# Three of eight sample-attention chains moved into the last prompt-attention phase, their loads reordered, and the later tokens' outputs computed first

## What is computed

```python
h = rmsnorm(x, pre_w)
q_sb, k_sb, v_sb, g_sb, q_dl, k_dl, v_dl, g_dl = in_projection(h, w_in)   # 1024 -> 4096
# stick-breaking: a = exp(log_sigmoid(z) + sum over later keys of log_sigmoid(-z))
o_sb = stick_breaking(q_sb, k_all, v_all, q_pos, sb_b)
# dilated: three windows with ALiBi, joined by their denominators
o_dl = combine_by_denominator(outs, lses)
y = concat(headnorm(o_sb) * silu(g_sb), headnorm(o_dl) * silu(g_dl))
m = einsum('bte,ed->btd', y, w_out)                                       # 1024 -> 1024
y_out = x + rmsnorm(m, post_w)
```

## Time and profile before

| what | us |
|---|---|
| three runs, median (lowest, highest) | 1068.59 (1066.04, 1073.83) |
| profiled execution, device time | 1075.81 |
| its span in the trace | 1074.0 |
| PE busy | 978.9 |
| DVE busy | 559.3 |
| ACT busy | 456.9 |
| POOL busy | 341.6 |

### The profile page before, as it was taken

One profiled execution on the slowest core, in us unless ns is written; L12 is line 12 of the kernel. 1 busy time (PEld: TensorE's weight loads), 2 busy tenths in 40 slices (PEclk: granted clock), 3 DMA queues, 4 the chain that ended last, 5 costly groups with the idle time before them and its releaser, 6 DMA issues.

```text
span 1074.0 us, 16718 instructions
## 1 busy us (share of the span) xinstructions
PE 978.9 (91%) x5590; PEld 847.7 (79%) x5590; DVE 559.3 (52%) x1000; ACT 456.9 (43%) x885; POOL 341.6 (32%) x271
## 2 busy tenths in 40 slices
PE   4999999999989999999999999899974279999995
PEld 3988789898878989978898988789663268888874
DVE  5556666655756665566666657666861012222121
ACT  6335465445546543544554346454552012222121
POOL 3244542223454222345422324540345001122101
PEclk9999999999999999989999999999685689999797
DMA  8111011111011111100121110001235635243511
GB/s 244 54 58 42 27 42 54 47 53 42 21 30 39 53 48 54 41 23 23 40 60 48 51 39 27 16 26 41 90 109 224 225 104 160 92 135 103 148 68 39
DMA packets 97276, 76.19 MB, mean 71 GB/s; under 512 B 7267, under 2 KB 91491, under 8 KB 97059
## 3 DMA queue, kind: packets, MB, share of 16 engines
q1 hardware_dynamic: 96034, 70.89, 21.4%
q10 hardware_dynamic: 1152, 4.19, 1.3%
HBM read 61.69 MB, written 21.76 MB: 78 GB/s over the span
## 4 chain that ended last, share of the span: by engine, by line
PE 49%; SPq 18%; issue 13%; ACT 6%; DVE 6%; POOL 5%; DMA 2%; POOLq 0%; DVEq 0%; ACTq 0%
PE proj_bank L628 10%; PE proj_bank L630 9%; PE proj_bank L629 9%; SPq L534 6%; SPq L525 5%; SPq L527 5%; PE sc_bank L716 4%; PE sc_bank L735 4%; PE sc_bank L720 3%; POOL work L1505 2%; PE o_bank L755 2%; PE sc_bank L721 2%; PE o_bank L756 2%; PE sc_bank L788 1%; DVE work L1311 1%
## 5 line engine op out<-in xcount | busy, mean ns | idle before, releaser
L628 PE MATMUL proj_bank<-h_hi,w_hi 128*128 128x384 f32 (+1 forms) x768 | 280.8, 366 | 0.0
L630 PE MATMUL proj_bank<-h_hi,w_lo 128*128 128x384 f32 (+1 forms) x768 | 253.8, 330 | 0.0
L629 PE MATMUL proj_bank<-h_lo,w_hi 128*128 128x384 f32 (+1 forms) x768 | 253.0, 329 | 0.0
L1279 DVE TENSOR_TENSOR split<-sc_bank,split 128x512 fp32r<-128x512 f32 (+1 forms) x160 | 101.8, 636 | 150.2 <-ACT split L997 149.3
L628 PEld LDWEIGHTS proj_bank<-h_hi,w_hi 128*128 128x128 f32 x768 | 146.0, 190 | 23.1 <-issue 17.9
L629 PEld LDWEIGHTS proj_bank<-h_lo,w_hi 128*128 128x128 f32 x768 | 146.6, 191 | 3.4 <-issue 3.4
L997 ACT ACTIVATE split<-sc_bank 128x512 fp32r<-128x512 f32 (+1 forms) x160 | 87.8, 549 | 136.6 <-PE sc_bank L735 134.3
L630 PEld LDWEIGHTS proj_bank<-h_hi,w_lo 128*128 128x128 f32 x768 | 145.9, 190 | 0.0
L1505 POOL TENSOR_TENSOR work<-work 128x896 f32<-128x896 f32 (+3 forms) x64 | 97.9, 1534 | 121.6 <-DVE work L1311 121.6
L1311 DVE TENSOR_TENSOR_SCAN work<-work 128x896 f32<-128x896 f32 (+3 forms) x64 | 95.8, 1497 | 18.1 <-ACT work L1012 18.1
L735 PE MATMUL sc_bank<-consts,work 128*128 128x128 f32 x576 | 92.8, 280 | 10.4 <-DVE split L1279 8.1
(11 more groups left out here) (162 smaller groups left out, 1699.0 us busy)
## 6 DMA issues: line engine op xcount, KB each, us to landing
w_raw<-in_w_in_dram SPq DMA_DIRECT2D x64, 256.0 KB, 2.9
out_dram<-stage SPq DMA_DIRECT2D x32, 192.0 KB
gated<-in_x_prompt_dram SPq DMA_DIRECT2D x8, 512.0 KB, 9.3
wo_raw<-in_w_out_dram SPq DMA_DIRECT2D x8, 512.0 KB, 3.5
kc<-in_cache_k_sb_dram SPq DMA_DIRECT2D x64, 64.0 KB, 1.9
vc<-in_cache_v_sb_dram SPq DMA_DIRECT2D x64, 64.0 KB, 1.9
kc<-in_cache_k_dil_dram SPq DMA_DIRECT2D x32, 128.0 KB, 2.3
vc<-in_cache_v_dil_dram SPq DMA_DIRECT2D x32, 128.0 KB
```

Source lines behind the costliest of these rows:

```text
L628: mm(o, w_hi[:, s, k, :], h_hi[:, k, c0:c0 + n_all], start=(k == 0), stop=False)
L629: mm(o, w_hi[:, s, k, :], h_lo[:, k, c0:c0 + n_all], start=False, stop=False)
L630: last = mm(o, w_lo[:, s, k, :], h_hi[:, k, c0:c0 + n_all], start=False, stop=(k == NK - 1))
L1279: ve.tensor_tensor(a_lo[:, k % 2, 0:n], turn_bank(name, ("T", k))[:, 0:n], a_hi[:, k % 2, 0:n].bitcast(F32), ALU.subtract).then_inc(low_se ...
```

## The change

1. **Chains 0, 1 and 2 run inside phase 8.** Each starts at a step of `CHAIN_AT` = 5, 17, 29 and is spread over ten steps on PE, ACT and DVE (`early_chain`). Their key transposes use the sc_bank tiles 2 and 3, in turn with the transposes of the probabilities ("KT" entries in `TURNS`); scores and sums use proj_bank. Nothing is taken out of phase 7: its gates are still projected there ("late" has the same units as "main").
2. **The output stage** has five tiles with a chain (3 to 7) and then three plain ones and the sample tile. Tiles are of tokens 4, 5, 6, 7, 0, 1, 2, 3, since the norm of the later 512 tokens is done first: its M sum is at step 38 of phase 8, the other one in the first tile.
3. **Loads.** The page table is loaded at the start and read once into 16 registers after phase 7's last stores; the two window copies are issued by ACT behind the first prompt table, before the attention begins. On SP: page keys of chain 0 (after phase 7's scores), page values (after its values), mask and table, window keys of chain 1, then `w_out` in 16 halves woven between the loads of chains 1, 2 and 3 (chain 2's keys wait for chain 0's transposes, its values for chain 0's end, chain 3's keys for chain 1's transposes), each half behind the split of the half two before it. POOL splits halves, all 16 ahead of its next `square_chunk`. Loads for chains 3 and 4 wait for chains 1 and 2.
4. **Tiles in SBUF.** The per-group pairs (`w_hi`, `q_hi`, `k_hi`, `v_st`, ...) become two tensors each and are laid out so that each chain's tiles lie over tensors no longer in use; `us` and `zs` are one tile. Loops of the output stage are unrolled, and the bias is read from `bias_all` without a copy.

The diff, cut to its core:

```diff
-K_LOADS, V_LOADS = (16, 8), (17, 10)
+K_LOADS, V_LOADS = (16, 8), (17, 9)
+TOKENS = [4, 5, 6, 7, 0, 1, 2, 3]
+NEARLY = 3
+CHAIN_AT = [5, 17, 29]
-SHARE = {..., "last": [[LAST_AT[s]] if s in LAST_AT else [] for s in range(NS)]}
+SHARE = {..., "late": shares(UNITS, False), "last": [last_units(s) for s in range(NS)]}
+        for j in range(NEARLY if name == "last" else 0):
+            if 0 <= s - CHAIN_AT[j] < 2:
+                out += [("KT", 4 * j + 2 * (s - CHAIN_AT[j]) + x) for x in range(2)]
...
@@ block.sync @@
-            for b in range(2):
-                sp.dma_start(wo_raw[:, b], wo_view[:, b, :]).then_inc(wo_in[b], 16)
             sp.wait_ge(pages_in, 16)
+            page_of = [sp.value_load(pages[0:1, n:n + 1], min_val=0, max_val=n_pool - 1) for n in range(16)]
...
-            load_paged(0, 0)
+            sp.wait_ge(copied, NROWS * 7)
+            for b in range(2):
+                sp.wait_ge(stage_out[b], 64 * 8)
+            load_keys(0)
+            sp.wait_ge(summed, NSTEPS * 7)
             load_paged(0, 1)
-            for e in range(2, 8):
-                sp.wait_ge(wo_set, e - 1)
-                sp.dma_start(wo_raw[:, e % 2], wo_view[:, e, :]).then_inc(wo_in[e % 2], 16)
-            for kv in range(2):
-                sp.dma_start(win_out[kv][:, 0:win, :], win_rows[kv]).then_inc(rows_out, 16)
+            sp.dma_start(s_mask[:], c_sample_mask).then_inc(mask_in_s, 16)
+            load_terms(0)
+            sp.wait_ge(big_done, NBIG * 7 + 9)
+            sp.wait_ge(w_set, 64)
+            load_keys(1)
...
+            load_wo(2)
+            load_new(0, 0)
+            load_new(0, 1)
+            load_windows(0, 1, 1)
+            load_keys(2, 1)
+            load_values(2, 1)
+            load_keys(3, 1)
+            load_wo(16)
+            sp.wait_ge(copied, NROWS * 8)
+            residual_in(0)
+            residual_in(1)
+            load_values(3)
+            load_keys(4)
+            sp.wait_ge(summed, NSTEPS * 8)
+            sp.dma_start(post_row[:], ...).then_inc(post_in, 16)
+            load_values(4)
...
@@ block.tensor, attention, at the end of each step s @@
+                    if units == "last":
+                        for j in range(NEARLY):
+                            early_chain(j, s - CHAIN_AT[j])
+                        if s == 38:
+                            small_group(2 * NPAIR + 1, "M", 0, None, None)
+            def early_chain(j, x):
+                if 0 <= x < 2:
+                    turn_early(j, 2 * x)
+                    turn_early(j, 2 * x + 1)
+                if x == 2:
+                    sample_scores(j, lambda n: None)
+                if j % 2 == 0 and x == 5:
+                    sample_sums(j)
+                if j % 2 == 1 and x == 4:
+                    sample_turn(j, False)
+                if j % 2 == 1 and x == 6:
+                    sample_turn(j, True)
+                if x == 7 + j % 2:
+                    sample_values(j, proj_bank[:, 1, 384:512], lambda n: None)
...
+            turn_keys(NEARLY, (0, 1))
+            turn_keys(NEARLY, (2, 3))
+            pe.wait_ge(wo_set, 16)
+            for n in range(8 - NEARLY):
+                sample_tile(n)
+            for n in range(8 - NEARLY, 9):
+                start_output(n)
+                output(n % 2, 0, 48)
...
@@ block.scalar @@
             load_table(0, 0)
+            for kv in range(2):
+                act.dma_start(win_out[kv][:, 0:win, :], win_rows[kv]).then_inc(rows_out, 16)
             attention("dl", -1, "first", None, first=LEAD_FROM)
...
@@ block.vector, called at the end of each step of phase 8 @@
+            def early_chain(j, x):
+                if j == 0 and x == 0:
+                    dve.wait_ge(summed, NSTEPS * 7)
+                    ve.memset(q_bd[:], 0.0)
+                    ve.memset(ones_f[:], 1.0).then_inc(consts_set, 1)
+                    dve.wait_ge(consts_set, 3)
+                    dve.wait_ge(mask_in_s, 16)
+                    prepare(0)
+                if x == 2:
+                    sample_terms(j)
+                    prepare(j + 1)
...
@@ block.gpsimd @@
-            for e in range(8):
+            pool.wait_ge(big_done, NBIG * 8)
+            for m in range(16):
...
-            for j in range(2):
-                square_chunk(2 * NPAIR + 1, j)
+            square_chunk(2 * NPAIR + 1, 0)
+            low(0)
+            square_chunk(2 * NPAIR + 1, 1)
```

More of the change, by code:

```diff
@@ L158, in shares @@
     return [[]] * start + out
-SHARE = {"first": shares(UNITS_FIRST[FIRST_V:], True), "main": shares(UNITS, False), "last": [[LAST_AT[s]] if s in LAST_AT else [] for s in range(NS)]}
+SHARE = {"first": shares(UNITS_FIRST[FIRST_V:], True), "main": shares(UNITS, False), "late": shares(UNITS, False), "last": [last_units(s) for s in range(NS)]}
 def finished(units):
@@ L646, in bank_free @@
                     pe.wait_ge(tv_set, 3 * ph + j + 1)
+                elif what == "KT":
+                    pe.wait_ge(kct_set, j + 1)
                 else:
@@ L757, in values, with turn_group, turn_early @@
                 last.then_inc(summed, 1)
+            def turn_group(j, g, bank):
+                for n in range(4 * g, 4 * g + 4):
+                    last = mm(bank[:, (n % 4) * P:(n % 4) * P + P], kcs[j % 2][:, n, :], ident, start=True,
+                              stop=True, is_transpose=True)
+                last.then_inc(kct_turned, 1)
+            def turn_early(j, g):
+                if g == 0:
+                    pe.wait_ge(k_in[j % 2], K_LOADS[j % 2] * 16 * (j // 2 + 1))
+                bank_free(2 * NPAIR, "last", "late", TURNS["last"].index(("KT", 4 * j + g)))
+                turn_group(j, g, turn_bank("last", ("KT", 4 * j + g)))
@@ new lines, in sample_turn, with sample_values @@
+            def sample_turn(j, back):
+                pe.wait_ge(s_dve, 5 * j + (4 if back else 1))
+                for x in range(3):
+                    last = mm(proj_bank[:, 0 if back else 1, x * P:x * P + P], (es if back else zs)[:, x, :], ident,
+                              start=True, stop=True, is_transpose=True)
+                last.then_inc(s_pe, 1)
+            def sample_values(j, bank, between):
+                br = j % 2
+                pe.wait_ge(s_act, 3 * j + 3)
+                pe.wait_ge(v_in[br], V_LOADS[br] * 16 * (j // 2 + 1))
+                o = bank.rearrange("p (h n) -> p h n", h=2)
+                mm(bank, v_new[:, br, :], us[0:NSAMP, 2, :], start=True, stop=False, skip_group_check=True)
+                for n in range(16):
+                    b = n // 2
+                    w = us[:, n % 2, :].rearrange("p (h n) -> p h n", h=2)[:, :, b * DS:b * DS + DS]
+                    last = mm(o[:, :, b * DS:b * DS + DS], vcs[br][:, n, :], w, start=False, stop=(n == 15), skip_group_check=True)
+                    if n == 15:
+                        last.then_inc(s_pe, 1)
+                    between(n)
@@ L1039, in attention @@
                             fold(ph, f)
+                    for j in range(NEARLY if last else 0):
+                        early_chain(j, s - CHAIN_AT[j])
+                    if last and s == 39:
+                        evacuate(2 * NPAIR + 1, 0, 0, (None, [("M", 0)]))
                     if kind == "sb" and s == 31:
@@ L1341, in attention @@
                             fold(ph, f)
+                    for j in range(NEARLY if last else 0):
+                        early_chain(j, s - CHAIN_AT[j])
                 if last:
+                    gate_chunk(2 * NPAIR + 1, 0, slice(7, 8))
                     fold(ph, 3)
@@ L1566, in _ @@
[L1566 to L1575 removed]
+            attention("sb", NPAIR - 1, "late", "main")
+            attention("dl", NPAIR - 1, "last", "late", last=True)
+            pool.wait_ge(big_done, NBIG * 8)
@@ new lines, in residual @@
+            def residual(n, rows=P):
+                b = n % 2
+                pool.wait_ge(out_norm, n + 1)
+                pool.wait_ge(x2_in[b], 8 * (n - b) + 16)
+                gp.tensor_tensor(m_out[0:rows, b], m_out[0:rows, b], x_out[0:rows, b], ALU.add).then_inc(out_sum, 1)
+            low(0)
+            square_chunk(2 * NPAIR + 1, 1)
+            low(1)
+            for n in range(8):
+                if n + 2 < 8:
+                    low(n + 2)
+                residual(n)
+            residual(8, NSAMP)
```

697 lines of the change are left out of this document (359 added, 338 removed).

## The result

| | median of 20 runs, us | lowest to highest |
|---|---|---|
| before | 1072.13 | 1064.61 to 1077.38 |
| changed | 1079.23 | 1070.45 to 1087.67 |

The ratio is 1.0062 (95%: 1.0038 to 1.0086): slower by 0.6%, where 5% faster was forecast. That is within the 1% that the prediction called no change, and outside its range of 988 to 1042 us. The profiled execution has a span of 1078.8 us, against 1074.0.

A forecast was written before the change was run, and what follows sets the result against it. Phases 1 to 7 PE-bound, then holes from late `w_out` and post-norm loads; phase 8 at 93.5 us ends at 845.7, tiles start at 849.7, span 1020, median about 1014 us (5% less), range 988 to 1042.

The forecast's parts named there:

- early copy, phase 1: Window copy started at about 56 us on ACT delays the weights of phase 1: 1 us, bounds 0 to 23.
- phase 8: PE's work (34.8 + 29): Phase 8: its own PE work at the upper clock, 34.8 us, plus three chains, 29 us (25.5 to 35).
- phase 8: PE idle (6.75 + 7.5 + 8.5): Phase 8: idle time as before 6.75 us, uncovered hand-overs of three chains 7.5, PE's stall for the late sample mask 8.5.
- between phase and tiles: Between phase 8 and the output tiles: chain 3's 16 transposes and the norm's way to the first low part, 4 us.
- tiles and end: Output stage: five chain tiles 113.4 us, M sum 1.1, four plain tiles 44.0, end 8.7, short waits 2.
- The clock: Phase 8: the 8.5 us stall drops PE's clock, 7 us lost (2 to 16).
- the clock stays low: Rival: over 54 us more PE work at the lower level loses the gain; 1116 us for phase 8 and two tiles; chance 0.05.
- the mask's stall: Phase 8, step 5: DVE waits for the sample mask, issued behind the page values; PE stands 8.5 us (0 to 18).
- Lower end, because the loads here are on another queue than the copy: Phase 1: reason for taking 1 us of a possible 23 for the early copy; weights were to land within the slack.
- Hand-overs: Phase 8: waits between a chain's parts on PE, ACT and DVE, 2.5 us a chain uncovered, 7.5 in all (0 to 15).
- a sign that I gave for being right: Sign that the forecast is right: no long POOL wait for `w_out`.
- chains in series: Rival: each chain lengthens phase 8 by a whole tile's 22.67 us, 126.8 in sum, total 1047 us; chance 0.09.

## Why the prediction was wrong

Most of the miss is one term, the 7 us put down to the clock in phase 8. The forecast for the profiled span was 1020 us, the measured one is 1078.8. By the forecast's own steps, in us:

| step | forecast | measured |
|---|---|---|
| early copy, phase 1 | 1 | 17.7 |
| phase 8: PE's work (34.8 + 29) | 63.8 | 69.0 |
| phase 8: PE idle (6.75 + 7.5 + 8.5) | 22.8 | 18.5 |
| phase 8: lower clock | 7 | 38.8 |
| between phase and tiles | 4 | 2.8 |
| tiles and end | 169.2 | 179.7 |

The differences add up to 58.7 us, the whole miss.

1. **The step that failed most is "The clock", the 7 us (2 to 16).** It was sized by the one stretch at half clock that phase 8 had before (14.5 us), as a price per stall. The runs show a loss that grows with the work put in, and faster than it: the stretch up to the tiles loses 11.6 us on 36.9 of work without chains, 18.8 on 48.3 with one, 37.0 on 68.8 with three. Phase 8 without chains is not alike from run to run either. Here it is in the kernel before with the copy in pieces, `w_out` late (the pieces spread, then the sixteen early ones) and `w_out` early:

```profile
748.70:798.50 49.80, 39.86 (x211) 31.05 (x210) 37.96 (x82) 25.93 (x57) 15.21 (x9) 0.86 0.31 96
```
```profile
754.70:813.00 58.30, 49.11 (x211) 38.76 (x210) 42.31 (x82) 25.92 (x57) 24.07 (x15) 0.68 0.33 105
```
```profile
748.20:803.20 55.00, 48.52 (x210) 38.09 (x210) 39.92 (x82) 26.04 (x57) 30.12 (x17) 0.68 0.36 116
```

The same work (34.3, 33.4 and 33.0 us) loses 5.6, 15.7 and 15.5 us to the lower level, and the phase is 49.8, 58.3 and 55.0 us long: a part of the loss goes into idle time, most of it does not. In the first two the code of phase 8 and its loads is the same. Their first 18.2 us agree to 0.01 us of PE work, a gap of 4.1 us of PE with them; behind it the clock is low for some 6 us in the one (767 to 773, and once more later), and for 35.6 without a break in the other, though PE is busy in 33.66 of them:

```profile
748.70:766.90 18.20, 11.92 (x66) 8.25 (x64) 16.74 (x33) 9.68 (x23) 8.45 (x5) 0.98 0.32 103
766.90:774.50 7.60, 7.60 (x29) 6.12 (x30) 4.92 (x10) 4.15 (x8) 0.00 (x0) 0.60 0.21 60
```
```profile
754.70:772.90 18.20, 11.92 (x67) 8.25 (x65) 16.75 (x33) 9.67 (x23) 8.46 (x5) 0.97 0.34 106
772.90:808.50 35.60, 33.66 (x123) 27.56 (x124) 23.07 (x46) 14.09 (x31) 11.28 (x7) 0.50 0.29 95
```

So a single stretch, like the 14.5 us that I took from the trace of before, could not size this term. My rival "the clock stays low" had the mechanism, but I asked of it 54 us and gave it 0.05; beside point 2, which took 17, some 37 us were enough. What keeps the clock down was not found. Taking the mask's stall away or adding matmuls left it at 0.64 to 0.68, and leaving 84 products out brought only 0.71. POOL's splits beside DVE are not needed for it: in the run with no chains and `w_out` late the clock fell at 769 us, with POOL idle since 758. PE has gaps of over 1 us in every phase 8 looked at, with chains or without (the longest 4.6), which no run here removed.
2. **"Lower end, because the loads here are on another queue than the copy" was the wrong choice.** The bounds (0 to 23) held, the value did not: the choice took the queue as a barrier, and a store on SP took 32.4 us beside a copy on ACT's. The weights alone were looked at; the chain that held PE goes through the row stores, whose stage buffers I had not listed among the DMAs beside the copy. The prediction took from the Trainium skill's page "DMA: Bandwidth & Descriptors", section "Queues, rings and completion order", that a DMA engine takes turns between its queue rows packet by packet, and concluded that the weights land within the slack. That conclusion is not what happened with DMAs of 4 MB, where the measurement decides: 17.7 us. The rule itself is not refuted by it. It counts packets, not bytes, and the copy's were of 58 KB beside 0.5; the prediction never asked for their size. With DMAs of 512 KB there was nearly no cost (1043.96 against 1040.7 for the spread pieces).
3. **What held.** The mask comes as late as forecast, and the run that removes it is 8.6 us faster for 8.5; but that it fits is partly luck, as that run also takes away a wait for the keys, which the prediction did not have (PE's two waits: 1.9 and 4.6 us in the changed kernel, 4.3 and 3.6 with the copy in pieces). A page at about 0.5 us: 0.54. A chain's work: 29 for three forecast with bounds of 25.5 to 35, measured 31.9 (34 by the changed kernel's own row, 69.0 less 34.8). Hand-overs: too dear by a few us. DVE had the room that the prediction gave it against the exclusion with POOL: 49.4 us busy of 126.4. No wait for the post-norm row or of PE for `w_out`, though POOL's waits for `w_out` (longest 17.8 us) go against a sign that I gave for being right; plain tiles 10.9 for 11.0; the end 8.9 for 8.7. The tiles' 10.5 us over the forecast are again the clock (12.9 us at 0.50, then 0.98) and 6 us of idle. The prediction read the slices of the page a little off: PE's hole is in slices 30 to 33, and the clock dips from 29 on. By luck phase 8 is as long as the rival "chains in series" had it, 126.4 for 126.8 us: PE is idle in only 18.5 of them, so waits between the parts of a chain are not what made it long.
4. **The framing.** The forecast put the gain of the change in one sum, 54 us. Taken apart, its own numbers had said that the chains give nothing: 3 x 11.7 saved, 29 + 7.5 spent. The gain was all in the two loads that stood in the way (`w_out` behind the pages, the post-norm row behind the copy), and those can be mended without moving a chain. That gives 1028.87 us, 4% below the kernel before and 50 us below the changed one, with none of the change's chains. The later tokens first, the registers and the unrolled loops add nothing to it (1029.35).

## What to carry to other kernels

Before work is moved into a phase because its engine idles there, ask at what clock the phase runs: if it is low already, added work costs more than its length (here 1.6 times for one chain and 1.8 for three, in the stretch itself), and it must beat the full price it saves elsewhere, not the idle time. Split a change in the sum into "loads mended" and "work moved" and give each its own total, since one can hide the other's loss. And try a large copy in the background in pieces first: in this kernel that was worth 15 to 32 us, early or late, on either queue.

## What the hardware showed beyond that

- Two DMAs of 4 MB and sixteen of 512 KB, same bytes, same queue, same place: a store beside the former took 28.9 us and the kernel 1058.6 us, beside the latter it took 1043.96. The DMA engines were idle in half of the slices in the first case (43.0% for the copy's queue), not in the second (51.6%).
- The same instructions can meet a different clock: 6 us at the lower level in one run and 36 in another, behind the same 18.2 us of the same phase. My estimate from the two (49.8 and 58.3 us long): a difference between single executions in such a phase is good to some 8 us only.
- In the changed kernel a run's time follows its mean clock: of 20 executions one at 0.941 had a span of 1068.6 us, one at 0.926 a span of 1082.1. It is no rule for every kernel: with one chain in phase 8 a run at 0.917 had 1037.7 us and one at 0.952 had 1045.7.
